# First modulation by feature halves: load order, row vectors and the first weight slab rearranged in a two-block transformer kernel

## What is computed

```python
def rms_norm(x, g):
    xf = x.astype(jnp.float32)
    y = xf * lax.rsqrt(jnp.mean(xf * xf, axis=-1, keepdims=True) + EPS)
    return (y * g.astype(jnp.float32)).astype(x.dtype)

def modulate(h, shift, scale):
    return h * (1.0 + scale[:, None, :]) + shift[:, None, :]
```

## Time and profile before

| what | us |
|---|---|
| median of 3 runs | 1524.01 |
| lowest and highest run | 1522.27, 1524.06 |
| span of the profiled execution (first to last instruction) | 1521.1 |
| PE busy | 1470.7 (97%) |
| DVE busy | 710.7 (47%) |
| ACT busy | 408.3 (27%) |
| POOL busy | 865.7 (57%) |

### The profile page before, as it was taken

The page is one execution under the profiler, slowest core; times in us unless marked ns, Lnnn a source line. Parts: engine busy times, 40 slices in busy tenths (PEclk is TensorE's granted clock), DMA queues, the critical chain, the costliest instruction groups (busy, mean ns, idle before and its releaser), DMA issues.

```text
span 1521.1 us, 18613 instructions
## 1 busy us (share of the span) xinstructions
PE 1470.7 (97%) x7119; PEld 1194.5 (79%) x7119; DVE 710.7 (47%) x1063; ACT 408.3 (27%) x829; POOL 865.7 (57%) x333
## 2 busy tenths in 40 slices
PE   3999999999999999999999999999999999999997
PEld 3788777778888888888898844789689888888886
DVE  6997156553741122112253886441517444454446
ACT  3101133332520111102243376452414111211113
POOL 1857453435755656565568996365154656565651
PEclk9999999999999999999999999999999999999999
DMA  9775222232323232323242300133023232322231
GB/s 344 287 276 193 94 83 70 70 111 83 111 98 110 83 111 83 111 84 111 83 147 92 97 6 1 59 135 112 0 84 106 89 104 90 102 91 101 93 101 66
DMA packets 91912, 162.45 MB, mean 107 GB/s; under 512 B 3469, under 2 KB 44353, under 8 KB 91841
## 3 DMA queue, kind: packets, MB, share of 16 engines
q1 hardware_dynamic: 88720, 155.20, 30.0%
q10 hardware_dynamic: 3121, 6.26, 1.3%
HBM read 159.35 MB, written 2.10 MB: 106 GB/s over the span
## 4 chain that ended last, share of the span: by engine, by line
PE 85%; DVE 8%; ACT 3%; DMA 2%; issue 1%; POOL 0%; DVEq 0%; SPq 0%; ACTq 0%; POOLq 0%
PE bank L708 26%; PE bank L709 26%; PE bank L710 26%; DVE bank L1690 2%; DMA ada_w<-in_w_ada 1%; DVE smx L2056 1%; PE bank L1117 1%; DVE x L1686 1%; DVE bank L1686 1%; PE bank L1187 1%; PE bank L1168 1%; PE bank L961 1%; PE bank L984 1%; ACT junk L1280 1%; PE bank L1144 0%
## 5 line engine op out<-in xcount | busy, mean ns | idle before, releaser
L623 POOL TENSOR_TENSOR w_lo<-w_raw,w_hi 128x2048 fp32r<-128x2048 f32 x119 | 553.9, 4654 | 9.9
L621 POOL TENSOR_SCALAR w_hi<-w_raw 128x2048 fp32r<-128x2048 f32 x119 | 231.6, 1946 | 565.8 <-DMA w_raw<-in_w_in 112.9
L708 PE MATMUL bank<-ht_hi,w_hi 128*128 128x512 f32 (+1 forms) x1200 | 443.2, 369 | 1.0 <-DVE ht_lo L1686 1.0
L709 PE MATMUL bank<-ht_hi,w_lo 128*128 128x512 f32 (+1 forms) x1200 | 440.3, 367 | 0.0
L710 PE MATMUL bank<-ht_lo,w_hi 128*128 128x512 f32 (+1 forms) x1200 | 440.0, 367 | 0.0
L708 PEld LDWEIGHTS bank<-ht_hi,w_hi 128*128 128x128 f32 x1200 | 226.5, 189 | 42.6 <-DVE ht_lo L1686 2.9
L710 PEld LDWEIGHTS bank<-ht_lo,w_hi 128*128 128x128 f32 x1200 | 226.5, 189 | 37.0
L709 PEld LDWEIGHTS bank<-ht_hi,w_lo 128*128 128x128 f32 x1200 | 226.6, 189 | 36.6 <-issue 0.5
L1690 DVE SCALAR_TENSOR_TENSOR uc<-bank,par,uc 128x511 f32<-128x511 f32 x88 | 66.0, 750 | 167.7 <-ACT uc L1656 166.2
L1686 DVE TENSOR_TENSOR facc<-bank,facc 128x512 f32<-128x512 f32 x104 | 72.0, 692 | 118.4 <-PE bank L710 110.5
L1656 ACT ACTIVATE uc<-bank,par 128x512 f32<-128x512 f32 x44 | 34.4, 781 | 257.6 <-PE bank L710 249.8
(11 more groups left out here) (258 smaller groups left out, 2000.4 us busy)
## 6 DMA issues: line engine op xcount, KB each, us to landing
w_raw<-in_w_in SPq DMA_DIRECT2D x27, 1024.0 KB, 5.0
ada_w<-in_w_ada SPq DMA_DIRECT2D x48, 512.0 KB, 7.4
w_raw<-in_w_up SPq DMA_DIRECT2D x22, 1024.0 KB, 4.9
w_raw<-in_w_mlp_in SPq DMA_DIRECT2D x16, 1024.0 KB, 5.2
w_raw<-in_w_mlp_out SPq DMA_DIRECT2D x16, 1024.0 KB, 4.9
w_raw<-in_w_down SPq DMA_DIRECT2D x11, 1024.0 KB, 4.9
w_raw<-in_w_out SPq DMA_DIRECT2D x8, 1024.0 KB, 5.0
w_raw<-in_w_mem_kv SPq DMA_DIRECT2D x8, 1024.0 KB, 5.2
```

What stands on the lines that cost most here:

```text
L621: g.tensor_scalar(w_hi[:, r], w_raw[:, r], 1.0, 1.0, ALU.mult, ALU.mult).then_inc(slab_hi, 1)
L623: g.tensor_tensor(w_lo[:, r], w_raw[:, r], w_hi[:, r].bitcast(F32), ALU.subtract).then_inc(slab_split, 1)
L708: inc_free(pe.matmul(o, ah, bh, start=start, stop=False))
L709: pe.matmul(o, al, bh, start=False, stop=False)
```

## The change

- Pieces 0 to 7 now hold shift and scale of features 0 to 511 (two runs of 2 KB for each partition instead of one of 4 KB), pieces 8 to 15 those of features 512 to 1023. `first_sums(0)`, `first_mod(0)` and chunks 0 to 3 need only the first eight pieces.
- The blocks of x are loaded behind pieces 0 to 3, and the reciprocals stand behind products 1, 2, 3 and 5.
- The sixteen small vectors move from ACT's queue to SP's, eight behind piece 4 and eight behind piece 5. PE turns them after all rows of x, and DVE copies them after product 7 instead of 11.
- Slab 0 is loaded behind piece 7, slab 1 behind piece 15, without the wait for all sixteen. `split_first` waits for eight used pieces.
- PE begins slab 0 after the first half. The sums of the second half and the transposes of chunk 7 stand behind the 48 matmuls of slab 0 (`second_sums`). DVE does products 8 to 15 after `first_low(3)`.

```diff
-X_WITH = (5, 7, 9, 11)
-NORM_WITH = (7, 9, 11, 13)
-VEC_WITH = 11
+X_WITH = (0, 1, 2, 3)
+NORM_WITH = (1, 2, 3, 5)
+ROWS_WITH = (4, 5)
+VEC_WITH = 7
...
-TILES = [("cvec", 1), ("vec", 1), ("nt1", DC - 2), ("ada01", 2), ("nt1_last", 2), ("w_in", 24), ("ada25", 6), ("pconv", 8), ("att1", 10 * H1 + PAIRS),
+TILES = [("cvec", 1), ("vec", 1), ("nt1", 4), ("ada0", 1), ("nt1b", 3), ("ada1", 1), ("nt1_last", 1), ("w_in", 24), ("ada25", 6), ("pconv", 8), ("att1", 10 * H1 + PAIRS),
...
                 s = i // DC
-                sp.dma_start(ada_w[:, r], wada[:, i % DC, s * D:(s + 1) * D]).then_inc(ada_loaded[r], 16)
-
+                if s < 2:
+                    two = wada[:, i % DC, 0:2 * D].rearrange("p (j n) -> p j n", j=2)[:, :, 512 * s:512 * s + 512]
+                    sp.dma_start(ada_w[:, r].rearrange("p (j n) -> p j n", j=2), two).then_inc(ada_loaded[r], 16)
+                else:
+                    sp.dma_start(ada_w[:, r], wada[:, i % DC, s * D:(s + 1) * D]).then_inc(ada_loaded[r], 16)
...
             for i in range(2 * DC):
                 ada(i)
                 if i in X_WITH:
                     m = X_WITH.index(i)
                     sp.dma_start(x[:, m], A["x"][m * P:m * P + P, :]).then_inc(x_loaded[m], 16)
-            win = w_rows(A["w_in"])
+                if i in ROWS_WITH:
+                    for to, of in row_vectors[8 * (i - ROWS_WITH[0]):8 * (i - ROWS_WITH[0]) + 8]:
+                        sp.dma_start(to, of).then_inc(rows_loaded, 16)
+                if i % DC == DC - 1:
+                    load(raw4, win[:, 4 * n:4 * n + 4, 512:1024])
             i = 2 * DC
-            for c0 in (512, 1024, 0, 1536, 2048, 2560):
+            for c0 in (1024, 0, 1536, 2048, 2560):
                 for s in range(2):
-                    if n == 1:
-                        sp.wait_ge(ada_used, 2 * DC)
                     load(raw4, win[:, 4 * s:4 * s + 4, c0:c0 + 512])
-                    for _ in range(4 if n > 2 else 0):
+                    for _ in range(4):
...
                 g.wait_ge(slab_loaded[0], 16)
-                g.wait_ge(ada_used, 2 * DC)
+                g.wait_ge(ada_used, DC)
...
             for m in range(NT):
-                if m == 1:
-                    turn_rows()
-                if m == NT - 1:
-                    first_sums(0)
                 first_rows(range(DC - 2), m)
-            first_sums(1)
-            for c in (DC - 2, DC - 1):
+            turn_rows()
+            first_sums(0)
+            for m in range(NT):
+                first_rows((DC - 2,), m)
+
+            def second_sums():
+                first_sums(1)
                 for m in range(NT):
-                    first_rows((c,), m)
-            features(T0["w_in"], 2, ht_hi, ht_lo, each=lambda k: Tile(NT1_T[k]).wait_taken(pe), first=True)
+                    first_rows((DC - 1,), m)
+
+            features(T0["w_in"], 2, ht_hi, ht_lo, each=lambda k: Tile(NT1_T[k]).wait_taken(pe), first=True,
+                     behind={(0, 3): second_sums})
...
-            for i in range(2 * DC):
+            for i in range(DC):
                 ada_product(i)
...
-            first_mod(0)
-            first_affine(0)
-            first_mod(1)
-            first_low(0)
-            first_affine(2)
-            first_low(1)
-            for pair in range(1, DC // 2):
-                if pair + 1 < DC // 2:
-                    first_affine(2 * pair + 2)
-                first_low(2 * pair)
-                first_low(2 * pair + 1)
+            for half in range(2):
+                if half:
+                    ada_products(1)
+                first_mod(half)
+                first_affine(4 * half)
+                first_affine(4 * half + 2)
+                for c in range(4 * half, 4 * half + 4):
+                    first_low(c)
             ada_products(2)
             ada_products(3)
```

More of the change, by code:

```diff
@@ L90 @@
 AFTER_FILLED = (1, 0, 5, 4, 2, 6, 3, 7)
+AFTER_ADA0 = 6
 CONV_BANK = {"conv31": BANKS - 1, "conv31_pe": BANKS - 2}
@@ L104, in banks_of_tiles @@
                 b, at = ROPE_BANKS[name][k], BANKS - 4
-            elif name == "nt1_last":
-                b = bank[-2]
+            elif name in ("ada1", "nt1_last"):
+                b = AFTER_ADA0
             elif name in FILLED:
@@ L242 @@
 NB = {"nt1": 0, "memnt": NT, "nt2": NT + MT, "nt3": 2 * NT + MT, "nt4": 3 * NT + MT, "nt5": 4 * NT + MT}
-NT1_T = [TILE0["nt1"] + c for c in range(DC - 2)] + [TILE0["nt1_last"] + c for c in range(2)]
+NT1_T = [TILE0["nt1"] + c for c in range(4)] + [TILE0["nt1b"] + c for c in range(3)] + [TILE0["nt1_last"]]
 def turned(name, m, h):
@@ L501, in ada @@
                 s = i // DC
-                sp.dma_start(ada_w[:, r], wada[:, i % DC, s * D:(s + 1) * D]).then_inc(ada_loaded[r], 16)
+                if s < 2:
[3 more added lines that the diff above has]
+                    sp.dma_start(ada_w[:, r], wada[:, i % DC, s * D:(s + 1) * D]).then_inc(ada_loaded[r], 16)
+            row_vectors = []
+            at = 0
+            for name in ("g_pre_mix", "g_pre_mlp", "conv_w", "norm_mix_pre_2", "norm_mem_pre_2", "mem_norm_g_2",
+                         "norm_ffn_pre_2", "conv_dw_b_2", "conv_ln_g_2", "conv_ln_b_2", "c", "b_ada"):
+                v = A[name].rearrange("(r p) -> r p", p=P)
+                row_vectors.append((rows[at:at + v.shape[0], 0, :], v))
+                at += v.shape[0]
+            assert at == P
+            fd = A["ffn_dw_2"].rearrange("(r p) -> r p", p=P)
+            row_vectors += [(rows[0:K2 * CC, 1, :], A["conv_dw_2"].rearrange("(r p) -> r p", p=P)), (rows[0:88, 2, :], fd[0:88]),
+                            (rows[0:44, 3, :], fd[88:132]), (rows[44:88, 3, :], A["ffn_dw_b_2"].rearrange("(r p) -> r p", p=P))]
+            win = w_rows(A["w_in"])
             for i in range(2 * DC):
@@ L894, in first_sums @@
             def first_sums(s):
+                t = Tile(T0[f"ada{s}"])
+                t.wait_free(pe)
                 pe.wait_ge(ada_used, DC * (s + 1))
                 for c in range(DC):
[L898 to L901, removed]
+                    at = DC * (c // 4) + 4 * s + c % 4
                     ins = pe.matmul(t.ap[:, at:at + 1], ada_acc[:, s, c * P:c * P + P], ones[:, 0:1], start=True,
                                     stop=True)
-                    if s == 1 and c % 4 == 3:
-                        ins.then_inc(t.full, 1)
+                ins.then_inc(t.full, 1)
             def modulation(s):
@@ L1255, in _ @@
             act.dma_start(c_row[:], A["c"].rearrange("(r p) -> r p", p=P)).then_inc(c_loaded, 16)
[L1256 to L1267, removed]
             def load_ada_b(j, s):
@@ L1385, in _ @@
                 if pair % 2 == 0:
-                    Tile(T0["ada01"] + pair // 2).wait_taken(act)
+                    Tile(T0[f"ada{pair // 2}"]).wait_taken(act)
                 t = Tile(NT1_T[c])
@@ L1821, in first_mod @@
             def first_mod(half):
-                t = Tile(T0["ada01"] + half)
+                t = Tile(T0[f"ada{half}"])
                 t.wait_full(v)
```

## The result

| | before | after |
|---|---|---|
| median of 6 runs each, same chip, us | 1524.03 | 1533.24 |
| lowest and highest | 1522.27, 1525.34 | 1528.48, 1533.49 |
| span of the profiled execution | 1521.1 | 1531.7 |

The ratio is 1.0057, with a 95% interval of 1.0047 to 1.0068. The changed kernel is slower, by about twice what I had forecast, and beyond the range. Its runs form two groups: two of six near 1529, four near 1533.3. The profiled execution (1533.39) is of the second; of the first there is no trace.

What follows compares the result with a forecast made beforehand. PE's stream was taken to bound the kernel from the first dense matmul, behind a DMA-full head. The 58th matmul's shift of +4.4 us, with no further loss, on the median 1524.0 gave 1528.4; range 1522.8 to 1531.0.

Steps and rivals of the forecast that it cites:

- First half: Start through slab 0: product 7 ends at 22.0, product 8 starts at 31.7; PE is 11 us ahead.
- Second half: Products 8 to 15 to the 58th matmul: the lead is given back, 58.75 against 53.55, +3.7 to +5.2, taken as +4.4.
- The pattern taken from 130 us: Eight products beside POOL's split of a slab take 16.1 us instead of 10.5, two of them 2.74 and 5.44.
- the bound of 5.2: Upper end of the 58th matmul's delay, with the nine matmuls on chunks 4 to 6 at low clock.
- the arrival of slab 1: Slab 1 comes 6.64 us after the piece's issue by the rows; the skill page's estimate is 5.6.
- DVE behind it ... No further loss.: DVE's later products up to group 4: starting 10.4 us later leaves 2.8 to 4.8, about PE's own shift.
- PE's wait for a bank at group 4: Sign at group 4: if PE waited for a bank there, the forecast would be wrong.
- rival 3: SP's sixteen issues run the queue dry, or clock stays low behind the second start: 1 to 3 us more, chance 0.11.
- Rivals 1 and 2: POOL misses the products: near 1524.5, chance 0.22; or the same with fast sums and DVE catching up: 1520.5, chance 0.07.
- DVE is a floor: At group 4's first bank: DVE can't run ahead, so PE can gain hardly more than its 0.45 us of slack.
- x ahead: Loads before piece 7: two blocks of x counted among its 12 units of 512 KB at 1.37 us each.
- The vectors on SP: Sixteen row vectors ahead of piece 7 in SP's queue: between nothing and 1.4 us, taken as 0.8.

Runs made afterwards that it cites:

- e2: The changed kernel with POOL's split of slab 1 held back until all 16 products are done: median 1527.98 us, ratio 1.0036.
- e1: The changed kernel with ACT's three 512 KB loads issued once 14 products are done, instead of behind the last chunk: 1528.85 us, ratio 1.0035.
- e10: The kernel before with one wait added, so that ACT's three loads are issued only when slab 0 has been freed: 1529.88 us, ratio 1.0039.
- e5: The changed kernel with ACT's three loads early and the split of slab 1 behind product 15: 1528.03 us, ratio 1.0026.
- e6: The changed kernel with the sixteen row vectors back on ACT's queue: 1534.13 us, ratio 1.0075.
- e11: The changed kernel with ACT's loads early, slab 1 split behind all products, product 8 before first modulation, y earlier, slabs reordered on SP: 1522.14 us, ratio 0.9997.
- e8: The kernel before with only the loads of x moved behind pieces 0 to 3 and the reciprocals with them: 1525.58 us, ratio 1.0014.

## Why the prediction was wrong

**First half: right.** Product 7 ended at 21.91 (forecast 22.0), product 8 started at 31.28 (31.7), PE's first matmul at 28.94 (29.3), slab 0 was done at 41.2.

**Second half: right.** The pattern taken from 130 us came again: 2.74 and 5.33, the end at 47.28 (47.8). The sums took 3.55 at the low clock, `first_mod(1)` came at 51.01 (51.55), and the 58th matmul at 58.35 (58.75), against 53.67 in the trace of before. The full shift was 5.3, not 4.4, because the clock stayed low to 59.5, past that matmul; the bound of 5.2 had left that out. e2 gives the price of the two blocked products by itself: 5.4.

For the arrival of slab 1 the row's 6.64 was the better price: piece at 32.07, POOL's start at 38.50, 6.43. The Trainium skill's estimate of 5.6 (DMA: Bandwidth & Descriptors, anatomy of one DMA) was 0.8 short here; the page gives that fit for loads issued by GpSimd, and these are issued by SP. PE's granted clock was at its lower level (0.50, 1.2 GHz) from 45.9, some 4 us after the last matmul of slab 0 (41.21), and the sums at 47.43 ran at it. The Trainium skill (TensorE: Matmul & The Clock Gate, Part 1) calls this the state of an idle array, and the trace agrees.

**The step that failed: "DVE behind it ... No further loss."** It was priced at 0 and measured 5.5. PE's wait for a bank at group 4, which the prediction names as a sign of being wrong, came. The main error: I did not count ACT's three loads among what the later chunks move; they went from 43.6 to 54.3 and met slab 3 (4.4 us of wait on DVE; e1 takes the loss away, e10 makes it in the kernel before). DVE's delay at `yt_lo`, which I took as 2.8 to 4.8 against PE's own, was 9.4 with the meeting (136.02 against 126.65); without it, in e1, it was 5.0, so that sum was nearly right. And I counted what POOL takes from DVE as a total, where it goes by single products: part of what the meeting costs comes that way (2.3 of 4.35 us in e1), and so does all of e5's delay against e2. Having written that the slack was 0.45 us, I should have given a loss there a chance of its own. Of rival 3 the dry queue is refuted by e6; its other half, a clock that stays low behind the second start, came, and made the first part 5.3 instead of 4.4. Rivals 1 and 2 did not come.

**The claim that DVE is a floor** ("PE can gain hardly more than 0.45") fits e5, where a shift of -1.4 became +6.2, and was got round in e11 by doing y earlier.

**The small terms.** x ahead had no term beyond its four units in the count; that was enough here (product 7 came as forecast), though in the kernel before, with sixteen products to go, e8 shows 1.4 us. The vectors on SP were taken as 0.8 of cost; e6 shows them 1.0 cheaper than on ACT.

## What to carry to other kernels

When a step moves, list what each engine does right behind it, its own DMA issues above all, and see on which transfers they now fall: 1.5 MB on another queue made a slab take 9.7 instead of 5.1 us. Where a second engine has less than a microsecond of slack somewhere downstream, a head start of the first is worth nothing until that place has been given room, and the stall goes from bank to slab to slab. If two engines lock each other out, count single instructions in the new phase, not a mean.

## What the runs showed that I had not expected

A wait of PE costs more than its length: around waits of 3.6 us (changed kernel), 4.5 (e5) and 5.5 (e10) the granted clock was low for 3.4, 6.8 and 6.8 us, and the stream lost 5.5, 7.6 and 7.5. And an earlier start of POOL can make DVE later with no idle time shown for it, only longer instructions (products 30 and 31 of e5: 2.74 and 5.43, where e2 has 1.28 and 2.75).
